# Spreading the running maximum's rows over the partitions by DMA, and two sets of score banks, in the mLSTM heads stage of a two-layer mixer and MoE kernel

## The reference

```python
b = jnp.cumsum(fc, axis=-1)
d = jnp.where(causal, b[..., :, None] - b[..., None, :] + ic[..., None, :], -jnp.inf)
inter = b + m[..., None]
m_t = jnp.maximum(inter, jnp.max(d, axis=-1))
s = jnp.einsum('bhtd,bhsd->bhts', qc, kc) * jnp.exp(d - m_t[..., None])
...
h = num / jnp.maximum(jnp.abs(den), jnp.exp(-m_t))[..., None]
```

## Time and profile before

| | us |
|---|---|
| median of three runs | 2103.58 |
| lowest, highest | 2100.83, 2109.34 |
| the profiled execution's own time | 2115.88 |
| its span, first to last instruction | 2114.2 |
| stage `mlstm_heads` in it | about 214.5 to 342.7 |

### The profile page before, as it was taken

One profiled execution on the slowest core, in us unless ns is written; L12 is line 12 of the kernel. 1 busy time (PEld: TensorE's weight loads), 2 busy tenths in 40 slices (PEclk: granted clock), 3 DMA queues, 4 the chain that ended last, 5 costly groups with the idle time before them and its releaser, 6 DMA issues. The chain is left out here.

```text
span 2114.2 us, 25835 instructions
## 1 busy us (share of the span) xinstructions
PE 1896.8 (90%) x9774; PEld 1614.1 (76%) x9774; DVE 1428.8 (68%) x1543; ACT 1001.4 (47%) x1125; POOL 113.2 (5%) x120
## 2 busy tenths in 40 slices
PE   7999986869999996899966759999999999999996
PEld 2677665658778885788856649898989898989895
DVE  2575365455454556576449448889898988888887
ACT  3323222342222223422344236777777767676765
POOL 1000011000000000000039000000000000000000
PEclk9999586989999998799987869999999999999998
DMA  7354110223433453344410029999999999999994
GB/s 252 111 191 156 31 40 1 80 91 130 168 122 127 156 179 114 100 150 140 160 40 1 0 88 332 319 354 318 338 333 336 338 332 334 328 345 328 340 331 167
DMA packets 245886, 412.27 MB, mean 195 GB/s; under 512 B 7689, under 2 KB 161457, under 8 KB 245691
## 3 DMA queue, kind: packets, MB, share of 16 engines
q1 hardware_dynamic: 244470, 411.25, 56.9%
q10 hardware_dynamic: 1350, 0.11, 0.0%
HBM read 410.29 MB, written 1.05 MB: 195 GB/s over the span
## 5 line engine op out<-in xcount | busy, mean ns | idle before, releaser
L2160 DVE TENSOR_TENSOR w_low<-e_ring,w_high 128x1408 fp32r<-128x1408 f32 (+2 forms) x384 | 617.4, 1622 | 103.6 <-ACT w_high L2097 100.8
L2097 ACT ACTIVATE w_high<-e_ring 128x1408 fp32r<-128x1408 f32 (+2 forms) x384 | 528.6, 1382 | 215.7 <-PE ps L2010 213.2
L2008 PE MATMUL ps<-w_high,list_h 128*128 128x352 f32 x1024 | 338.2, 330 | 18.0 <-DVE w_low L2160 16.4
L2010 PE MATMUL ps<-w_high,list_l 128*128 128x352 f32 x1024 | 329.8, 322 | 0.0
L2009 PE MATMUL ps<-w_low,list_h 128*128 128x352 f32 x1024 | 329.2, 322 | 0.0
L2008 PEld LDWEIGHTS ps<-w_high,list_h 128*128 128x128 f32 x1024 | 192.9, 188 | 26.7 <-DVE w_low L2160 25.8
L1305 ACT ACTIVATE fw_high<-ring 128x1024 fp32r<-128x1024 f32 x66 | 70.0, 1060 | 278.1 <-PE ps L1254 188.0
L1339 DVE TENSOR_TENSOR fw_low<-ring,fw_high 128x1024 fp32r<-128x1024 f32 x66 | 80.9, 1225 | 174.8 <-ACT fw_high L1305 174.8
L2009 PEld LDWEIGHTS ps<-w_low,list_h 128*128 128x128 f32 x1024 | 193.8, 189 | 0.3
L2010 PEld LDWEIGHTS ps<-w_high,list_l 128*128 128x128 f32 x1024 | 192.7, 188 | 0.0
L1252 PE MATMUL ps<-u_high,fw_high 128*128 128x512 f32 x352 | 140.3, 399 | 6.9 <-DVE fw_low L1339 6.9
(11 more groups left out here) (344 smaller groups left out, 3476.9 us busy)
## 6 DMA issues: line engine op xcount, KB each, us to landing
e_ring<-in_e_w_gu_dram SPq DMA_DIRECT2D x128, 1408.0 KB, 8.0
e_ring<-in_e_w_down_dram SPq DMA_DIRECT2D x32, 1536.0 KB, 7.3
bg_area<-in_mod_w_dram SPq DMA_DIRECT2D x80, 512.0 KB, 4.0
e_ring<-in_e_w_down_dram SPq DMA_DIRECT2D x32, 1280.0 KB, 7.6
ring<-in_f_w_gu_dram SPq DMA_DIRECT2D x22, 1024.0 KB, 7.1
ring<-in_h_w_in_dram SPq DMA_DIRECT2D x10, 2048.0 KB, 7.9
ring<-in_m_w_in_dram SPq DMA_DIRECT2D x6, 2048.0 KB, 7.9
ring<-in_f_w_down_dram SPq DMA_DIRECT2D x5, 2048.0 KB, 7.9
```

The costliest lines, as they stand in the source:

```text
L2008: nc.tensor.matmul(out, high[:, f, :], w_high[:, c, :], start=(f == 0), stop=False)
L2010: last = nc.tensor.matmul(out, low[:, f, :], w_high[:, c, :], start=False, stop=(f == total - 1))
L2097: nc.scalar.activation(piece(k.w_high, p), raw(p), ACT.Copy).then_inc(S.high_done, 1)
L2160: nc.vector.tensor_tensor(piece(k.w_low, p), raw(p), piece(k.w_high, p).bitcast(F32), ALU.subtract).then_inc(S.low_done, 1)
```

## The change

The matmuls of `spread_m` go from PE. In their place SP issues one DMA for each turn, which reads the turn's row of M (512 floats in one partition of `scan_m` or `scan_m_rev`) 128 times and writes it to the 128 partitions of one of four buffers in SBUF; the exponentials read these. The buffers lie in memory that the stage before used for `u_low`. The DMA of turn n waits from turn 4 on for the exponentials of turn n - 4, and the background's loads 18 to 23 are issued behind the DMAs of the turns 4, 6, ... 14. The two banks that become free, with bank 7, are a second set of score banks, used by the odd heads: scores(h + 1) is now issued at the turn 2h + 1, ahead of values(2h), and waits for the weighing of head h - 1 alone. Since bank 7 is also the background sum's, scores(1) waits for `k.bg.take`.

```diff
+M_SPREAD = 4
...
-    scored, spread, weighed, probs = k.sem("a_scored"), k.sem("a_spread"), k.sem("a_weighed"), k.sem("a_probs")
+    scored, weighed, probs = k.sem("a_scored"), k.sem("a_weighed"), k.sem("a_probs")
+    spread = [k.sem(f"a_spread{i}") for i in range(M_SPREAD)]
...
-    def score_cols(j):
-        return (j, 0) if j < 2 else (2, (j - 2) * 256 - 256)
+    def score_cols(h, j):
+
+        bank, col = (j, 0) if j < 2 else (2, (j - 2) * 256 - 256)
+        return ((0, 1, 2), (3, 4, 7))[h % 2][bank], col
+
+    def m_row(n):
+        return k.m_spread[:, n % M_SPREAD, :]
...
         @block.sync
         def _(sp):
-            for i in range(18, 24):
-                k.bg.load(sp, i)
+            def spread_m(n):
+                h, d = n // 2, n % 2
+                if n >= M_SPREAD:
+                    sp.wait_ge(weighed, 4 * (n - M_SPREAD + 1))
+                row = (k.scan_m, k.scan_m_rev)[d][8 * d + h:8 * d + h + 1, :]
+                sp.dma_start(m_row(n), row.unsqueeze(1).to_broadcast([1, P, T])).then_inc(spread[n % M_SPREAD], 16)
+
+            for n in range(turns):
+                spread_m(n)
+                if n >= M_SPREAD and n % 2 == 0:
+                    k.bg.load(sp, 18 + n // 2 - M_SPREAD // 2)
...
-                if h:
-                    pe.wait_ge(probs, 8 * h)
+                if h >= 2:
+                    pe.wait_ge(probs, 8 * (h - 1))
...
-            def spread_m(n):
-                h, d = n // 2, n % 2
-                if n >= 2:
-                    pe.wait_ge(weighed, 4 * (n - 1))
-                src = (k.scan_m, k.scan_m_rev)[d]
-                nc.tensor.matmul(k.ps[:, 3 + d, :], k.ident[0:16, 8 * d + h:8 * d + h + 1].to_broadcast([16, P]),
-                                 src[0:16, :], start=True, stop=True).then_inc(spread, 1)
...
             scores(0)
-            spread_m(0)
-            spread_m(1)
             k.bg.sum(pe, 1, 0, 7, 0)
             for n in range(turns):
-                if n % 2 == 0 and n:
-                    scores(n // 2)
-                    spread_m(n)
-                    spread_m(n + 1)
+                if n == 1:
+                    pe.wait_ge(k.bg.taken, k.bg.first_step[2])
+                if n % 2 and n < turns - 1:
+                    scores(n // 2 + 1)
                 if n:
                     values(n - 1)
...
-                act.wait_ge(spread, n + 1)
+                act.wait_ge(spread[n % M_SPREAD], 16 * (n // M_SPREAD + 1))
...
-                    nc.scalar.activation(decay[:, j, t0:t1], k.ps[:, 3 + d, t0:t1], ACT.Exp, scale=-1.0,
+                    nc.scalar.activation(decay[:, j, t0:t1], m_row(n)[:, t0:t1], ACT.Exp, scale=-1.0,
...
+        k.m_spread = at("m_spread", M_SPREAD * T, KD * T).rearrange("p (b t) -> p b t", b=M_SPREAD)
```

More of the change, by code:

```diff
@@ L922, in scores @@
             def scores(h):
-                if h:
-                    pe.wait_ge(probs, 8 * h)
+                if h >= 2:
+                    pe.wait_ge(probs, 8 * (h - 1))
                 base = (h % 2) * 64
                 for j in range(NT):
-                    bank, col = score_cols(j)
+                    bank, col = score_cols(h, j)
                     t0 = 0 if j < 2 else 256
```

## The result

The changed kernel has a median of 2119.99 us, against 2103.58 us before: **slower by 0.74%** (ratio 1.0074, 95% interval 1.0059 to 1.0089). The forecast was slower, 2152 us, in a range from 2083 to 2172.

What follows compares the result with a forecast made beforehand. A once-a-head loop DVE, PE, ACT, DVE was taken as the bound; shortening it saved 16.6 us, but sixteen spreads at 10.2 us ended the stage at 390.9 against 342.7: 2103.6 + 48.2 = 2152 us, range 2083 to 2172.

Steps and rivals of the forecast that it cites:

- The price of a spread: Time of one 256 KB DMA spreading a row of M: near end 0.64 us for the bytes, far end 10.2 us.
- The far end: Spread DMA's source: one partition served at a sixteenth of the full rate, 25.8 GB/s, 10.2 us a spread; the end taken.
- A: Main case: sixteen spread DMAs in one queue set the pace, +48.2 us, 2152 us, own range 2128 to 2172; chance 0.60.
- rival C: Spread DMAs at 6.5 to 7.8 us cancel the gain within 10 us, break-even 7.2 us, total 2104; chance 0.07.
- All of the 16.6 us is swallowed: Heads stage: the 16.6 us saved by moving spreads off PE and issuing scores early is lost to slow spread DMAs.
- 9.8 us a head, DVE with POOL's addition sets it: Heads at full clock, rows in time: two DVE turns of 4.14 us plus 1.5 us for POOL, instead of 11.5.
- (b) Scores go ahead: PE's order: scores issued a head early, ahead of values(2h), lie beside DVE's finish; part of the 16.6 us gain.
- Loads counted at nothing: SP's queue: six background loads between spreads cost nothing; in series they would add 7.6 us.
- 30 us and more: Spread DMAs in a full queue: time from DMA to landing, against about 12.9 us for the first.
- Its clock will be 0.50: PE in the heads stage idles more, so its granted clock falls to 0.50.
- The row at 201 GB/s: Two gain rows read repeatedly from DRAM with engines fully busy, taken as repetition halving the rate.
- Rival D: Heads stage: cheap DMAs but PE's clock stays at half throughout, +13 us, 2117 us; chance 0.04.

Runs made afterwards that it cites:

- e1: Changed kernel with all sixteen spreads reading partition 0 of the running maximum: 9.58 us a spread, whole kernel 2159 us.
- e0: The kernel before, unchanged, profiled a second time: span 2098.8 us, stage 115.6 us.
- e2: Changed kernel with each spread replaced by a 256 KB DMA from 128 partitions of the queries: 2089.43 us, ratio 0.993.
- e6: Changed kernel with the 16 rows of M written to DRAM and each spread reading its row there: 2088.96 us, ratio 0.9916.
- e17: Same kernel as e6 (rows through DRAM, two bank sets), measured on one chip with e15 and e16: 2090.3 us, ratio 0.9928.
- e10: Changed kernel with rows through DRAM but one set of score banks, scores after the previous head's last weighing: 2078.09 us, ratio 0.9861.
- e15: Same kernel as e10, measured on one chip with e16 and e17: 2078.86 us, ratio 0.9882.
- e14: Kernel before, with the next even turn's matmul spread moved ahead of the previous turn's values, no DMA: 2095.07 us, ratio 0.9939.
- e9: Changed kernel with the six background loads between spreads cut from 512 KB to 32 KB: the small loads took nothing off the stage.
- e16: Rows through DRAM and two bank sets as e6, but scores(1) behind values(0), on one chip with e15 and e17: 2088.03 us, ratio 0.9923.
- e5: Changed kernel with each row first copied to 8 partitions four apart, which its spread then reads: 2094.15 us, ratio 0.9936.
- e7: Changed kernel with spreads reading partitions 0 and 2 in turn: stage 169.2 us.
- e8: Changed kernel with spreads reading partitions 0, 4, 8 and 12 in turn: stage 132.0 us.

## Why the prediction was right, and where it was wrong

- **The price of a spread, the step that failed.** The far end was the right end: e1 has 9.58 us where I worked out 10.2, and the first spread landed after 12.4 us, forecast 12.9. Wrong was the term "16 x 10.2" = 163.2 us, spreads one after another. In the change neighbours read h and 8 + h and overlap in part: 7.18 us. Fifteen intervals, each 3.0 us shorter, and a first landing 0.5 us earlier bring the last row 45.8 us sooner; 2.8 us of that went into a later start and a longer tail, so the stage ended at 347.8 where I had 390.9. I had that overlap in the text, as the lower edge of A's own range, and gave it only 24 us; the result, 2120, lies below that edge. Nor was it true that only a read below 6.5 us could make the prediction wrong: the read takes 9.58 us, and the forecast failed all the same, on the overlap.
- **The price in effect was that of rival C.** 7.18 us a spread lies in C's band of 6.5 to 7.8, at my break-even of 7.2. By my own sum it ends the stage at 217.2 + 16 x 7.18 + 10.5 = 342.6, no change. The profile ends 5.2 us later, and that is all the loss that the first pair of profiles shows.
- **What it was counted against.** The stage of 128.2 us was a slow one; usual is 115.6 (e0). Against this the same mistake shows larger (176.4 forecast, +60.8 us; 132.9 measured, +17.3 us). The two errors partly cancelled. And a price at my break-even gave a clear loss only because the usual stage is 12.6 us shorter than the one I had broken even with: the right sign owes something to luck. I had noted the 12.3 us between the profiled execution and the median and carried them along as a constant, where they lay inside the stage that I was costing.
- **"All of the 16.6 us is swallowed"**: right. With rows in time the two-set stage is 100 to 104 us (e2, e6, e17), 11 to 15 us below the usual one, and the medians are 13 to 15 us below before. "9.8 us a head, DVE with POOL's addition sets it": 9.64 measured.
- **"(b) Scores go ahead"** as a part of the gain: wrong. The gain comes from the rows, which leave PE and are there ahead of time; e10 and e15 have it with one set, and more, and e14 has 0.6% from one row in time alone. I had both parts in the loop and did not ask which of them would still be late once the other was gone.
- **Loads counted at nothing**: right (e9). **DMA to landing "30 us and more"**: wrong, 17.5 us: by that time only some two spreads were under way at once (17.5 / 7.18 = 2.4), and SP stood in issuing the next. **"Its clock will be 0.50"**: wrong, 0.78 in the stage after, where before had 0.73 and 0.83 in its two profiles.
- **The row at 201 GB/s** as a sign that repetition halves the rate: not borne out. Two ordinary loads of 512 KB, issued from 51.66 us on, were in flight beside the two gain rows, and e6's repeated row lands in 4.5 us, as e2's does. In rival C, 256 KB in 6.5 us is 40 GB/s, not 43.
- Rival D, the half clock: not in the change, but it is the open remainder in e6, e16 and e17.

## What to carry to other kernels

Ask of a transfer not only how many bytes and engines it has but how many partitions it touches on each side: in a full queue, 256 KB from one partition took 9.6 us each (e1); from 128 partitions or from DRAM they landed in 4.5 us (e2, e6), and from 8 copies four apart they never kept ACT waiting after the first turn (e5). When two edits attack one loop, work out the loop with each edit alone; here half of the change, with a better source for the rows, beats the whole by about 2% and the kernel before by 1.2 to 1.4%. And when the profiled execution is off its median, find out where before costing the stage in which it may lie.

## What the runs showed of the hardware

- Partitions 0 and 2 share what limits a read (stage 169.2 us, as with one partition); neighbours in the queue from 0, 4, 8 and 12 overlap in part (132.0 us; e1, e7, e8). One partition gives 27.4 GB/s to all engines together, while the DMA share of e1's stage reads 0.83 at 47 GB/s, loads included: a busy share says nothing of bytes.
- An engine that issues DMAs is held while earlier spreads are under way, here some two by the time to landing: up to 8.9 us for the issue of a spread and 5.3 to 6.7 us for that of the loads in the steady part, where the same load's issue takes 0.33 us in an empty queue. Two queues overlap better than one (112.1 against 132.9 us, one execution).
- The clock's rise at the stage's start differs between executions of one kernel, and moves the stage by 12.6 us (128.2 and 115.6); what stands behind the stage takes 1771.5 or 1776.4 us in two profiles of one kernel (e17 and e6).
